# Retention half of the merge by seven half-size block products, with POOL adding the gated blocks

## The reference

```python
y_mla = mla_branch(...) * jax.nn.silu(gate_mla)                # 1024 x 1024
y_ret = retention_branch(..., g_ret[l]) * jax.nn.silu(gate_ret) # 1024 x 2048
merged = (jax.nn.sigmoid(merge_mla) * (y_mla @ w_proj_mla[l])
          + jax.nn.sigmoid(merge_ret) * (y_ret @ w_proj_ret[l]))
x = x + gate * (merged @ w_out[l])
return rmsnorm(x, g_final)
```

## Time and profile before

| what | us |
|---|---|
| runs | 1599.46, 1597.55, 1598.85; median 1598.85 |
| span of the profiled execution, first to last instruction | 1596.8 |
| PE busy | 1560.5 |
| DVE, ACT, POOL busy | 950.3, 615.3, 304.5 |
| from the first retention unit of the merge to the output product | 1327.4 to 1502.4 |
| from there to the end | 1502.4 to 1596.8 |

### The profile page before, as it was taken

How to read it: one execution, slowest core, us unless ns; L and a number is a source line. 1 busy time by engine, 2 the same in 40 slices (tenths; PEclk the granted TensorE clock), 3 DMA queues, 4 the chain that set the end, 5 groups by cost and what they waited for, 6 DMA issues and landing times. The chain is left out here.

```text
span 1596.8 us, 20305 instructions
## 1 busy us (share of the span) xinstructions
PE 1560.5 (98%) x7568; PEld 1304.3 (82%) x7568; DVE 950.3 (60%) x1625; ACT 615.3 (39%) x1068; POOL 304.5 (19%) x270
## 2 busy tenths in 40 slices
PE   5999999999999999999999999999999999999998
PEld 4788888888888888798888888887688888888886
DVE  6884444444444457752576665767878775647544
ACT  7553333333333343442343333434544444213111
POOL 0032332232222200200000000025555530000000
PEclk9999999999999999999999999999999999999999
DMA  9332332332233334799264554448967767345332
GB/s 382 106 135 107 112 112 106 117 121 106 106 112 108 97 95 166 308 412 331 90 210 168 179 196 169 172 162 286 320 211 244 241 215 264 122 152 170 136 106 79
DMA packets 142977, 280.67 MB, mean 176 GB/s; under 512 B 11280, under 2 KB 84112, under 8 KB 134176
## 3 DMA queue, kind: packets, MB, share of 16 engines
q1 hardware_dynamic: 126160, 246.92, 44.6%
q10 hardware_dynamic: 12080, 15.60, 2.9%
q0 software_dynamic: 4640, 16.84, 2.7%
HBM read 183.65 MB, written 94.63 MB: 174 GB/s over the span
## 5 line engine op out<-in xcount | busy, mean ns | idle before, releaser
L1638 DVE TENSOR_TENSOR w_form<-w_pair,w_form 128x512 fp32r<-128x512 f32 x150 | 116.1, 775 | 125.1 <-ACT w_form L1260 123.3
L1260 ACT ACTIVATE w_form<-w_pair 128x512 fp32r<-128x512 f32 x150 | 95.0, 634 | 240.7 <-PE p_banks L2168 235.7
L1335 ACT ACTIVATE prob<-p_banks,neg_max 128x128 f32<-128x128 f32 (+3 forms) x64 | 47.6, 743 | 182.9 <-DVE neg_max L1765 182.9
L2165 PE MATMUL p_banks<-h_hi,w_form 128*128 128x512 f32 x300 | 116.7, 389 | 0.0
L2167 PE MATMUL p_banks<-h_lo,w_form 128*128 128x512 f32 x300 | 116.7, 389 | 0.0
L2168 PE MATMUL p_banks<-h_hi,w_form 128*128 128x512 f32 x300 | 116.7, 389 | 0.0
L539 ACT ACTIVATE w_hi<-w_raw 128x1024 fp32r<-128x1024 f32 (+3 forms) x63 | 53.3, 849 | 140.7 <-PE p_banks L2423 96.8
L2423 PE MATMUL p_banks<-y_hi,w_lo 128*128 128x512 f32 x256 | 99.6, 389 | 0.0
L2422 PE MATMUL p_banks<-y_lo,w_hi 128*128 128x512 f32 x256 | 99.6, 389 | 0.0
L2421 PE MATMUL p_banks<-y_hi,w_hi 128*128 128x512 f32 x256 | 99.6, 389 | 0.0
L1077 POOL DMA_DIRECT2D v_ret<-v_stage x32 | 17.6, 550 | 398.9 <-DVE v_stage L1742 398.7
(11 more groups left out here) (320 smaller groups left out, 4285.9 us busy)
## 6 DMA issues: line engine op xcount, KB each, us to landing
w_pair<-in_w_pairs SPq DMA_DIRECT2D x25, 1024.0 KB, 4.9
w_raw<-in_w_dense SPq DMA_DIRECT2D x39, 512.0 KB, 4.8
v_ret<-v_stage POOLq DMA_DIRECT2D x32, 512.0 KB, 3.6
v_chunk<-v_ret SPq DMA_DIRECT2D x32, 512.0 KB, 3.7
merge_t<-act_t SPq DMA_DIRECT2D x48, 256.0 KB, 3.5
act_t<-stage SPq DMA_DIRECT2D x40, 256.0 KB, 2.0
act_t<-stage_late SPq DMA_DIRECT2D x40, 256.0 KB, 2.0
ada<-in_w_ada SPq DMA_DIRECT2D x4, 2048.0 KB, 24.9
```

What stands on the lines that cost most here:

```text
L1260: self.nc.scalar.activation(self.form[f % FORM_SLOTS][:, 0, :], self.form_source(f), ACT.Copy).then_inc(self.form_hi, 1)
L1335: nc.scalar.activation(self.prob[:, g % 2, 0:width], p[:, 6:8, :].rearrange("p a n -> p (a n)")[:, 0:width], ACT.Exp, bias=self.neg_max[:, ...
L1638: nc.vector.tensor_tensor(self.form[f % FORM_SLOTS][:, 1, :], self.form_source(f), self.form[f % FORM_SLOTS][:, 0, :].bitcast(F32), ALU.su ...
L2165: self.nc.tensor.matmul(out, w_hi[:, cut], x_hi[:, q, :], start=fresh and q == 0, stop=False, skip_group_check=True)
```

## The change

The retention half is now made by the Winograd form of Strassen's block scheme. The contraction is cut in even and odd heads, the tokens in even and odd chunks, the output columns in even and odd tiles of 128; then seven products of half-size blocks take the place of eight. The operands are blocks of `y_ret` and of the weights and sums of them:
- `tensor_merge` runs 28 units (seven products, 0 to 6, of four `quad`s), each again 24 matmuls of 512 columns (`ret_products`). Each unit has a weight tile of its own; before, two units shared one. Products 2 and 4 add onto the banks of products 0 and 1.
- The tokens' operands of a product are four tiles `t_raw` of 128 x 2 x 512, loaded, copied and lowered for each product (`high_t`, `low_t`), in two sets of four places. Before, 16 tiles were split once.
- The token sums are made by POOL during retention (`first_sums`, `other_sum`) from four `y_ret_stage` buffers and two `half_sum` buffers, and stored by SP to `t_sums`; for odd heads two halves are loaded back first.
- The weight sums of products 1, 3, 4 and 5 are made by POOL in the merge (`sum_weight`, 16 of them, 128 x 1024), partly with a second loaded block (`w_second`).
- After each unit DVE (`ret_outputs`) forms sums of products where the scheme asks for it and multiplies the finished blocks by the gate (`add_gated`, products 2, 4, 5, 6); POOL adds the 16 gated blocks to `merged` (`add_product`).
- The gain `g_ret` goes from the splits of `y_ret` to the retention gates, a second ACT copy on 32 half tiles in the projection stage.
- The output product takes the token tiles in the order 1, 3, 5, 7, 0, 2, 4, 6.

```diff
+SUMMED = (1, 3, 4, 5)
+GATED = (2, 4, 5, 6)
+GROUPS_SPLIT = ((0, 1), (2,), (3,), ())
+        for k in (CHUNK_STEPS - 3, CHUNK_STEPS - 1):
+            self.first_sums(pool, k)
+            self.other_sum(pool, k)
+        self.gpsimd_output(pool)
+    def first_sums(self, pool, k):
...
+        if k // NT % 2 == 0:
+            nc.gpsimd.tensor_tensor(even, odd, even, ALU.subtract).then_inc(self.t_sums_done, 1)
+            return
...
+        nc.gpsimd.tensor_tensor(half, odd, half, ALU.subtract).then_inc(self.t_sums_done, 1)
+        pool.wait_ge(self.t_sums_done, before + 1)
+        nc.gpsimd.tensor_tensor(even, half, even, ALU.subtract).then_inc(self.t_sums_done, 1)
+    def gpsimd_output(self, pool):
+        nc = self.nc
+        pool.wait_ge(self.yr_done, CHUNK_STEPS)
+        for u in range(RET_UNITS + RING):
+            if u < RET_UNITS and u // QUADS in SUMMED:
+                self.sum_weight(pool, u)
+            if u >= RING and (u - RING) // QUADS in GATED:
+                self.add_product(pool, u - RING)
+    def add_product(self, pool, u):
...
+        pool.wait_ge(self.merge_step, gated + 1)
+        self.nc.gpsimd.tensor_tensor(out, out, gate, ALU.add).then_inc(self.merge_added, 1)
+    def ret_outputs(self, dve, u):
...
+        dve.wait_ge(self.ret_summed, u + 1)
+        if product == 2:
+            self.add_gated(dve, u, bank)
+        elif product == 3:
+            dve.wait_ge(self.copied, COPIED_FROM + quad + 1)
+            nc.vector.tensor_tensor(first, bank, first, ALU.add).then_inc(self.second_sums, 1)
+        elif product == 4:
+            dve.wait_ge(self.second_sums, SECOND_SUMS_FROM + quad + 1)
+            nc.vector.tensor_tensor(bank, bank, first, ALU.add).then_inc(self.c_full, 1)
+            dve.wait_ge(self.c_full, C_FULL_FROM + quad + 1)
+            self.add_gated(dve, u, bank)
...
     def vector_output(self, dve):
         nc, p = self.nc, self.p
+        for u in range(RET_UNITS):
+            product, quad = divmod(u, QUADS)
+            self.ret_outputs(dve, u)
+            self.lower_weight(dve, R_RET + u + RING)
+            if product < RET_PRODUCTS - 1:
+                for g in GROUPS_SPLIT[quad]:
+                    self.low_t(dve, product + 1, g)
+            if 0 <= u - GATE_ROW_AT < KD:
+                self.weigh_gate(dve, u - GATE_ROW_AT)
...
+            if product >= 4:
+                self.low_merged(dve, u)
+            for k in OUT_SPLIT.get(u, ()):
+                self.lower_out_weight(dve, k)
+    def ret_products(self, pe, u):
...
+        pe.wait_ge(self.w_lo_ready, R_RET + u + 1)
...
+        for k in range(KD):
+            g, part = divmod(k, 2)
+            if quad == 0 and part == 0:
+                pe.wait_ge(self.t_lo_ready, T_FROM + T_GROUPS * product + g + 1)
```

More of the change, by code:

```diff
@@ L87 @@
 R_MERGE = len(SEQ)
-SETS = 3
 MERGE_LOAD = (1, 4, 5, 7)
@@ L1811, in merge_unit @@
         nc = self.nc
-        z_set, part = divmod(unit, 2 * KD)
-        tile, half = divmod(part, 2)
+        tile, half = divmod(unit, 2)
         gate = self.merge_t[:, unit % 2, :]
@@ L1835, in low_chunk, with add_gated @@
+    def add_gated(self, dve, u, block):
+        gated = self.gated_unit(u)
+        unit = 2 * KD + gated
+        gate = self.merge_t[:, unit % 2, :]
+        dve.wait_ge(self.t_loaded[unit % 2], 16 * (unit // 2 + 1))
+        self.nc.vector.scalar_tensor_tensor(out=gate, in0=gate, scalar=1.0, in1=block, op0=ALU.add, op1=ALU.mult)\
+            .then_inc(self.merge_step, 1)
     def low_chunk(self, dve, n):
```

693 lines of the change are left out of this document (449 added, 244 removed).

## The result

The changed kernel takes 1619.86 us (median of 4 runs, 1617.69 to 1622.02) against 1599.15 for the kernel before (4 runs, 1597.55 to 1600.86): a ratio of 1.013, 95% interval 1.0116 to 1.0144. That is slower by 20.7 us, and outside the range forecast. The profiled execution took 1622.0 us, its span is 23.4 us longer than that of before. Of the executions behind this document one, of `small_token_dmas` further down, took 3133.7 us, with matmuls of 675 ns at a recorded clock of 1.00, where the other three of that kernel took 1613.6 to 1616.2: its cause is open, it is the one that was profiled, and so that row has no times by stage.

The account below looks back on a forecast made before the run. It took PE alone to bound the merge; -21.8 (matmuls) + 17.5 (PE's waits for DVE and POOL) + 1 (start) + 1.5 (retention) = -1.8 us, so 1597.1 us; own range 1592 to 1602, eight-in-ten range 1583 to 1608.

Parts of the forecast that it names:

- PE's saving: Merge: 96 fewer matmuls at 0.2267 us each, 21.8 us less.
- The mechanism in the merge: Merge: POOL's operations and DVE's with two SBUF inputs exclude each other, alternate and lengthen DVE's turns beyond PE's 5.44 us.
- the turns in products 4 and 5: DVE per unit: product 4 8.1 us, first 9.4 to 11.3, last 7.2; product 5 7.4, 7.3, 8.3, 5.6.
- The places of PE's waits: Merge: PE waits for late weights and last operands, before units 16, 23 and 24 and within products 5 and 6.
- the sum of PE's waits in the merge: Merge: PE's waits for DVE's late weights and operands add up to 16.6 to 18.5 us, taken as 17.5.
- a rival (3, chance 0.08, 1603 to 1609): Merge: operand loads stand behind SP's waits, first operands land 3 us later in products 4 and 5; chance 0.08.
- the retention, 1.5 forecast: Retention: added POOL sums and 48 SP transfers cost 1.5 us, span 0 to 9.
- the upper bound of 9: Retention, odd heads: 9 us lost if only 0.9 of DMA time can be used, 63.2 us needed in head 1.
- Rival 2: Retention, odd heads: late half loads delay POOL's sums and rotations, a wait in 8 step pairs; about 1602 to 1603.6, chance 0.13.
- the start, 1 forecast: Start of product 0: operands load only behind step 30's y, then DVE lowers one; 1 us, span 0.5 to 3.
- The upper bound of 3: Start of product 0: 3 us lost if operand loads land 8.4 us after issue.

Follow-up runs that it names:

- small_token_dmas: Changed kernel with token-sum stores and half loads cut to 16 rows of 128 numbers, POOL's sums kept full size: 1615.70 us, ratio 1.0087 to 1.0121.
- small_pool_sooner: Changed kernel with POOL's weight sums on 8 columns, additions on 2 of 128, and operand loads ahead of the weight load: 1594.49 us, merge 155.7.
- sums_write_only: Changed kernel with each POOL weight sum replaced by two zero fills of the same 1024 columns, reading no SBUF: 1606.97 us, merge 169.9.
- filled_waits: Changed kernel with 20 extra PE matmuls before the long waits in units 12, 20 and 24: 1620.05 us, merge 181.9.
- small_pool_all: Changed kernel with POOL's weight sums on 8 of 1024 columns and additions on 2 of 128, waits and loads kept: 1596.18 us, merge 161.0.
- operands_first: Changed kernel with SP's four operand loads of product 0 moved ahead of the last half's load and its wait: 1619.81 us, merge 184.3.

## Why the prediction was wrong

**PE's saving** was right: 672 matmuls at 0.2267 are the floor that small_pool_sooner comes to within 3.4 us.

**The mechanism in the merge** was right: DVE and POOL alternate, for the sums sums_write_only shows that it is their reading, and the turns in products 4 and 5 came within 0.7 us of the forecast but for the first, which waited for its operands. The places of PE's waits were not. Forecast were 4.0 before unit 16, 3.5 to 5.4 in unit 20, 1.7 and 2.0 before units 23 and 24, and 5.4 in unit 24; measured were 6.4 in unit 12, which it did not have, 2.2, 6.2 and 5.4 at the first, second and last, and nothing before 23 and 24. Product 6 began 21.9 us late (12 to 14 forecast) and ended 29.8 us late (16 to 19).

**The first step that failed: the sum of PE's waits in the merge, 17.5 us, which should have been 29.5.** The walk through DVE's turns gave how late DVE is against a PE at its full rate. Measured, that lateness is 20.2 us of gaps and 9.3 us of matmuls that ran at the lower clock behind them. That the gaps alone come near 17.5 is luck. The slow matmuls are no term of their own to be added either: filled_waits took 3.8 of the 9.3 away, and the merge stayed as long, as DVE and POOL set the time. By small_pool_all, 21.1 of the merge's 29.8 us over its matmuls are POOL's operations, by small_pool_sooner another 5.3 late operand loads; 3.4 are left.

**The second, inside that sum: loads that come late.** The working took the operand loads as landing in time but for up to 1.9 us in product 4's first turn, and the gates' tiles as landing in time; lateness of the operands was left to a rival (3, chance 0.08, 1603 to 1609), whose mechanism is part of what happened. The trace has operand loads issued 8 and 16 us after their buffers are free, behind a weight load that waits for DVE itself, and a gate's tile behind the gate row's load. DVE waited 15.4 us for operands and 4.5 for the gate's tile. It is the latter that made most of unit 12's wait: with the gates' load first 6.4 us became 2.0 and the merge 4.6 shorter; with the operands' loads sooner it is 4.2 shorter.

**The third: the retention, 1.5 forecast.** 11.5 us were lost up to the last transposes in the profiled execution: 9.0 between steps 0 and 31, and 2.5 ahead of step 0. Over the other versions it is 4.7 to 8.5 between the steps. That the upper bound of 9, from DMA time in the odd heads, is of this size is luck: its 63.2 us of DMA time in head 1's 62 were 53.9 (a share of 0.87), head 1 lost 1.8 us (steps 8 to 16, 59.9 to 61.7) and head 3 none. Rival 2's chain of half loads is there on POOL, which waits 29.6 us for `half_sum` (L1266), 8.9 of them in head 3, where PE loses nothing; so it does not cost what the rival says in each pair of steps. What the sum had nothing for is head 0, 4.1 us, where the token sums hold DVE as the weight sums do in the merge, and head 2, 3.2 us. The 5.0 us of heads 1 and 2 stay with small operations and go when the transfers are small too. Where between steps 14 and 20 these bite stays open, and so does the scatter of 0.2 to 3.6 us ahead of step 0.

**The fourth: the start, 1 forecast, 4.9 measured.** The upper bound of 3 took the landing time, but not SP's wait for the store of a token sum, landed at 1337.1, ahead of the loads. operands_first gives this 1.6 us; the rest is not explained.

In all: -21.8 + 20.2 + 9.3 + 4.9 + 11.5 is 24.1, less the 0.9 us that the merge before had before its own gate row: 23.2 of the 23.4 in the span. The forecast had -1.8. The profiled execution is 2.2 us above its median, and the medians differ by 20.7. Every term of loss came out larger than its value, and none smaller, while the range let them offset each other.

## What to carry to other kernels

Giving POOL additions to relieve DVE buys nothing while both read SBUF: here the 16 additions cost the merge 5.0 us more on POOL than on DVE, and the 16 sums the same on either. Where an engine's turns are near PE's pace, follow the loads that its own progress releases: a transfer queued behind a wait on that engine turns one late turn into a late product. Where another engine sets the time, compare its lateness with PE's gaps and slow matmuls together, and don't expect filler work on PE to win it back. And place a loss by steps before naming its cause: here head 1, for which most DMA time was forecast, lost 1.8 us, and head 0 4.1.

## What the runs showed of the hardware

In the changed kernel 8 to 13 matmuls stood 0.43 us apart (1.2 GHz in place of 2.4) behind each of the gaps of 5.2 to 6.4 us, and 3 behind the one of 2.2; the granted clock was 0.90 in 1460 to 1526 us, and 1.00 there with the waits filled. The Trainium skill (TensorE: Matmul & The Clock Gate, section "Part 1: The HAM clock gate") has an idle array's clock halved; the 0.43 beside 0.227 agrees. A fill of 128x1024 by POOL takes 0.96 us and does not wait for DVE. In the kernel before, 57600 DMA packets of 512 bytes took 28 ns each on average, 291 GB/s if all 16 engines did only such; those of 2048 to 4096 bytes reached 357 to 358. This is what the prediction's 288 estimated from one stretch.
